# A second layer that takes unscaled rows, with the first modulation's gate steps moved to the first hybrid layer

## The chip, the core and the metric

The kernel runs on one core of one Trainium2 chip. The metric is the device time of one execution in microseconds (us), the median over runs. Everything is computed in float32; each large product is made of three fast ones, since both factors are split into a high half (rounded to fp32r) and a low half.

## The reference

256 rows of width 1024 go through four layers, each x + f(norm(x)) @ w_out, and a last norm. Layer 0 holds stick-breaking attention and an S5 mixer, layer 1 gated linear attention (GLA), layers 2 and 3 (the two hybrids) dilated attention and retention. What the change touches:

```python
def rms_norm(x, g):
    y = xf * lax.rsqrt(jnp.mean(xf * xf, axis=-1, keepdims=True) + EPS)
    return (y * g).astype(x.dtype)
# layer 1
h = rms_norm(x, odd_norm_g[i]);  proj = h @ odd_w_in[i]
q, k, v, z, r = jnp.split(proj, ...)
log_a = jax.nn.log_sigmoid(r @ gla_w_gate[i] + gla_b_gate[i]) / GLA_TAU
o = rms_norm(gla_chunked(q, k, v, log_a), gla_o_norm_g[i])
x = x + (o * jax.nn.silu(z)) @ odd_w_out[i]
# hybrids l = 0, 1
shift, scale, gate = jnp.split(c_act @ w_ada[l] + b_ada[l], 3)
h = rmsnorm(x, norm_w[l]) * (1 + scale) + shift
...
return x + gate * (merged @ w_out[l])
```

The factor of rms_norm is one number per row (token), so rows that aren't multiplied by it give products that can be multiplied by it afterwards.

## The kernel before

**Tiles and stream.** The 256 rows are two tiles (ti 0, 1) of 128 partitions. All weights come as one stream of 306 pieces, each two k-chunks of 128 rows by up to 512 columns (512 KB). SyncE loads piece n into RAW (five buffers) once the low half of piece n-5 is made; ScalarE (ACT) makes the high half WH (`hi(n)`, three buffers, after piece n-3 is read by TensorE), VectorE (DVE) the low half WL = RAW - WH (`lo(n)`, L1514); TensorE (PE) multiplies: for each chunk and row tile three matmuls of 512 columns (L598 to L600; L607 to L610 where the result is wanted turned). `half(time)` is one chunk of a piece, and time = 2n and 2n+1 are the steps by which everything else is placed: each engine's program is written out by hand as a loop over time, and the AT_ tables say at which step a side operation stands in it. hi and lo run two pieces ahead (AHEAD). Pieces 0 to 53 are layer 0, 54 to 89 layer 1, 90 to 197 and 198 to 305 the hybrids; the first pieces of layer 1 are `zr` (54 to 57, 336 columns), then gv0, gv1, gk, gq, z0, z1.

**From layer to layer.** The last three pieces of a layer (`closing`) run row tile by row tile (`split_half`, L636 to L638), so tile 0 is complete three halves ahead of tile 1; the first three pieces of the next (`opening`) do the same. In between, for each tile, DVE adds the product to X (`residual`, L2088), ACT squares X with a sum (`square`, L1091, which writes its squares to TK), DVE computes the factor NR by an inverse square root of 9 or 10 small dependent instructions (`rstd`, L1558 to L1574), DVE and GpSimd (POOL) multiply X by it into HN, which is TK (`scaled`, L1579, L2344), PE transposes HN (`norm_turn`, L699, four blocks to a bank), ACT takes the high halves HTh out of PSUM with the norm's weight as scale (`turned`, L1040) and DVE the low ones HTl (`turned`, L1590). The order on ACT and DVE is that of their `next_layer`, on PE that of `open_layer`.

**Modulations.** The hybrids' scale and shift columns are 16 dot products on DVE for each (`dot`, L1904, over w_ada_t, loaded by SyncE into two buffers): for the first hybrid at the steps AT_ADA0 in layers 0 and 1, for the second at AT_DOT1 in the first hybrid. The gate row is made of 16 gate steps on POOL (`ada`: load 256 KB, L2352, multiply, L2364 or L2366, add, L2368), at AT_ADA0 too for the first, at AT_ADA1 in the second hybrid for the second. After 8 steps each, PE sums over partitions with a matmul by ones (`ada_sum`, L812) and DVE adds the bias (`ada_out`, L1914).

**Layer 1's results.** ACT takes r (16 columns) and tanh(z/2) out of the zr banks, v out of gv0 and gv1, tanh(z/2) out of z0 and z1; DVE takes k and q with the decays; `gla_values` on ACT takes squares and copies of o (L1288), and DVE makes the norm of o (gr) and multiplies (`gla_gate`, L1979). In the hybrids DVE's `att_scores` (L2030 to L2037), ACT's `att_exp` and PE's `att_turn` (L900) follow one another for each of four heads, at steps 73 to 95.

## Time and profile before

| | |
|---|---|
| median of 3 runs | 1065.96 us (1065.74 to 1066.08) |
| the profiled execution | 1067.14 us |
| its span, first to last instruction | 1065.3 us |
| mean granted TensorE clock | 0.988 |
| busy: PE | 1017.6 us (96%) |
| busy: DVE, ACT, POOL | 708.7, 557.8, 205.2 us |
| DMA moved | 192.15 MB, mean 180 GB/s |

A busy PE isn't a PE at its peak, since matmuls overlap; but an idle PE is time lost wherever the chain that ended last runs through it. So the profile is read for the places where PE waits, and for what each of those waits hangs on.

### The profile page before, as it was taken

How to read it: one execution, taken by the hardware profiler on the slowest of the kernel's cores; microseconds unless marked ns; L12 is line 12 of the kernel's file. 1: busy time of each engine (PE TensorE's matmuls, PEld its weight loads, DVE VectorE, ACT ScalarE, POOL GpSimd, SP SyncE). 2: the span in 40 equal slices, each digit the busy share in tenths (PEclk: the TensorE clock that was granted, in tenths of full speed). 3: DMA queues.
4: the chain of work that ended last, by engine and by line, in shares of the span. 5: the costliest groups of instructions: out<-in, count | busy, mean ns of one | idle time of the engine just before them, and what ended most of it. 6: DMA issues, size and time to landing. Idle time of an engine off the chain costs nothing.

```text
span 1065.3 us, 15218 instructions
## 1 busy us (share of the span) xinstructions
PE 1017.6 (96%) x6020; PEld 891.8 (84%) x6020; DVE 708.7 (67%) x1113; ACT 557.8 (52%) x859; POOL 205.2 (19%) x212
## 2 busy tenths in 40 slices
PE   6999999989999899999999999989999999999996
PEld 5778889767977679998899888867999888998884
DVE  7984847978859656775566586664444565667666
ACT  6668577447435555445553345455444555334543
POOL 5800160423431100000004100020466000320000
PEclk9999999999999899999999999999999999999998
DMA  7543435758854568974466545545777446654651
GB/s 260 180 127 109 139 100 163 277 175 268 253 174 159 189 178 290 306 253 119 138 180 177 158 142 184 188 137 167 234 236 240 123 119 178 183 153 141 195 179 39
DMA packets 95350, 192.15 MB, mean 180 GB/s; under 512 B 8576, under 2 KB 11904, under 8 KB 95280
## 3 DMA queue, kind: packets, MB, share of 16 engines
q1 hardware_dynamic: 91008, 178.08, 54.2%
q0 software_dynamic: 3408, 11.18, 3.1%
q10 hardware_dynamic: 864, 1.93, 0.5%
q8 instruction: 47, 0.77, 0.3%
q14 instruction: 23, 0.19, 0.1%
HBM read 189.59 MB, written 1.05 MB: 179 GB/s over the span
## 4 chain that ended last, share of the span: by engine, by line
PE 83%; DVE 11%; ACT 3%; issue 2%; DMA 0%; DVEq 0%; ACTq 0%
PE G L598 14%; PE G L600 14%; PE G L599 14%; PE G L607 8%; PE G L610 8%; PE G L609 8%; DVE WL L1514 3%; PE B L561 2%; DVE AR L1904 1%; PE G L636 1%; PE G L638 1%; PE G L637 1%; ACT WH L1040 1%; PE B L900 1%; DVE SM L1572 1%
## 5 line engine op out<-in xcount | busy, mean ns | idle before, releaser
L1514 DVE TENSOR_TENSOR WL<-RAW,WH 128x1024 fp32r<-128x1024 f32 (+2 forms) x306 | 383.6, 1256 | 249.7 <-ACT WH L1040 248.7
L1040 ACT ACTIVATE WH<-RAW 128x1024 fp32r<-128x1024 f32 (+2 forms) x306 | 320.2, 1050 | 288.0 <-PE G L600 150.6
L598 PE MATMUL G<-WH,HTh 128*128 128x512 f32 (+1 forms) x564 | 228.3, 405 | 9.8 <-DVE WL L1514 9.5
L607 PE MATMUL G<-HTh,WH 128*128 128x256 f32 x768 | 219.5, 286 | 0.3 <-DVE HTl L1590 0.3
L600 PE MATMUL G<-WL,HTh 128*128 128x512 f32 (+1 forms) x564 | 218.4, 387 | 0.0
L609 PE MATMUL G<-HTl,WH 128*128 128x256 f32 x768 | 218.0, 284 | 0.0
L610 PE MATMUL G<-HTh,WL 128*128 128x256 f32 x768 | 217.9, 284 | 0.0
L599 PE MATMUL G<-WH,HTl 128*128 128x512 f32 (+1 forms) x564 | 217.5, 386 | 0.0
L607 PEld LDWEIGHTS G<-HTh,WH 128*128 128x128 f32 x768 | 147.7, 192 | 1.7 <-issue 1.5
L609 PEld LDWEIGHTS G<-HTl,WH 128*128 128x128 f32 x768 | 147.7, 192 | 0.4 <-issue 0.2
L610 PEld LDWEIGHTS G<-HTh,WL 128*128 128x128 f32 x768 | 147.6, 192 | 0.0
L598 PEld LDWEIGHTS G<-WH,HTh 128*128 128x128 f32 x564 | 106.2, 188 | 34.2 <-DVE WL L1514 11.6
L600 PEld LDWEIGHTS G<-WL,HTh 128*128 128x128 f32 x564 | 105.9, 188 | 21.8
L599 PEld LDWEIGHTS G<-WH,HTl 128*128 128x128 f32 x564 | 106.4, 189 | 18.4 <-issue 0.5
L2386 POOL TENSOR_TENSOR AR<-AR 128x256 f32<-128x256 f32 x16 | 18.2, 1139 | 318.4 <-DVE AR L2000 317.2
L598 PE MATMUL G<-WH,YTh 128*128 128x512 f32 x184 | 74.2, 404 | 2.5 <-DVE WL L1514 2.5
L600 PE MATMUL G<-WL,YTh 128*128 128x512 f32 x184 | 72.5, 394 | 0.0
L599 PE MATMUL G<-WH,YTl 128*128 128x512 f32 x184 | 72.3, 393 | 0.0
L1040 ACT ACTIVATE AR<-B 128x512 f32<-128x512 f32 (+5 forms) x83 | 43.0, 546 | 46.3 <-PE B L945 22.4
L2352 POOL DMA_DIRECT2D AR<-in_w_ada_g x32 | 18.7, 584 | 170.4 <-PE G L610 61.9
L1904 DVE CUSTOM_DVE_ANT_0 AR<-AR,CB,SM 128x1024 f32<-128x1024 f32 x32 | 48.9, 1528 | 2.8 <-DMA AR<-in_w_ada_t 2.8
L2368 POOL TENSOR_TENSOR AR<-AR 128x512 f32<-128x512 f32 x28 | 49.9, 1781 | 2.3
(344 smaller groups left out, 1320.5 us busy)
## 6 DMA issues: line engine op xcount, KB each, us to landing
RAW<-in_w_in SPq DMA_DIRECT2D x176, 512.0 KB, 3.8
RAW<-in_even_w_in SPq DMA_DIRECT2D x40, 512.0 KB, 3.7
AR<-in_w_ada_t SPq DMA_DIRECT2D x32, 512.0 KB, 4.8
AR<-in_w_ada_g POOLq DMA_DIRECT2D x32, 256.0 KB, 4.0
RAW<-in_odd_w_in SPq DMA_DIRECT2D x16, 512.0 KB, 4.2
RAW<-in_w_proj_ret SPq DMA_DIRECT2D x16, 512.0 KB, 3.5
RAW<-in_w_out SPq DMA_DIRECT2D x16, 512.0 KB, 3.6
RAW<-in_even_w_out SPq DMA_DIRECT2D x12, 512.0 KB, 4.3
```

Of the source, the lines that this page charges most:

```text
L561: ins = nc.tensor.transpose(ps[:, 128 * k:128 * k + 128], src(ti, j), IDENT)
L598: nc.tensor.matmul(o, xh, wh, start=begins, stop=False)
L599: nc.tensor.matmul(o, xl, wh, start=False, stop=False)
L600: ins = nc.tensor.matmul(o, xh, wl, start=False, stop=ends)
L607: nc.tensor.matmul(o, fh, h_[:, kx, :], start=begins and f % 2 == 0, stop=False, skip_group_check=True)
L609: nc.tensor.matmul(o, fh, l_[:, kx, :], start=False, stop=False, skip_group_check=True)
L610: ins = nc.tensor.matmul(o, fl, h_[:, kx, :], start=False, stop=ends and f % 2 == 1, skip_group_check=True)
L1040: return nc.scalar.activation(out_, ps, ACT.Copy, **kw)
L1514: vt(wl, raw, wh.bitcast(F32), ALU.subtract).then_inc(*dve.mark(LO, n))
L1904: nc.vector.tensor_tensor_reduce(w, w, CB[:, :], 0.5, co[f"b_ada{l}"][:, i:i + 1], ALU.mult, ALU.add, dst).then_inc(*dve.mark(DOT, l, i))
L2352: nc.gpsimd.dma_start((ADA2 if l else ADA)[:, i % 2, :], wv[:, i % 8, 512 * (i // 8):512 * (i // 8) + 512]).then_inc(s_ada[i % 2], 16)
L2368: gtt(acc, acc, w, ALU.add).then_inc(*pool.mark(ADA_P, l, i))
```

## The change

Layer 1 takes X as it is. `norm_turn(1, ...)` transposes X, right behind the residual sums; three of its four groups move into layer 0's last steps (AT_TURN1: after the halves 105, 106 and 107), the fourth behind the first half of layer 1. The squares, both `rstd` and a new `rows` (which makes NR squared, R2, and half of NR, HR) come at the end of `next_layer(1)` on ACT and DVE, ahead of lo(57) on DVE. The factor comes in where results leave PSUM: as scale of the copies of r, of tanh(z/2) and of v (there squared, for v and for k), of the squares and copies of o (for q), and once more in gr (for z). `scaled(1)` is gone on DVE and POOL, and with it TK as a stage.

The 16 gate steps of the first modulation and their two `ada_sum` go from layers 0 and 1 to the first hybrid, every fifth step from 25, sums at 63 and 104; the second modulation's dots there go from every third step to every fifth. The first modulation's dots stay (AT_DOT0 is the old AT_ADA0). The loads of ATM, DEC and GATE1, which ACT issued at the end of layer 1, and that of GATE0, which SyncE issued in layer 0, are issued by SyncE at step 12 of the first hybrid. POOL's three loads GM, RES and WGT, which followed `scaled(1)`, now wait until piece 55 is read. The gate steps' buffers are the second modulation's for both.

```diff
 AT_GLU_OUT = (89, 90)
-AT_ADA0 = (82, 86, 90, 94, 98, 112, 116, 120) + tuple(130 + 4 * i for i in range(8))
-AT_ADA0_SUM = {126: 4, 164: 5}
+AT_DOT0 = (82, 86, 90, 94, 98, 112, 116, 120) + tuple(130 + 4 * i for i in range(8))
 
...
+AT_DOT1 = tuple(27 + 5 * i for i in range(16))
+AT_ADA = [tuple(25 + 5 * i for i in range(16)), tuple(26 + 3 * i for i in range(16))]
+AT_ADA_SUM = [{63: 4, 104: 5}, {50: 4, 74: 5}]
+AT_LATE = 12
 AT_CB = 78
+AT_TURN1 = {105: (0, 0), 106: (0, 1), 107: (1, 0)}
+UNSCALED = (1,)
 
 
 
...
 
 
-        AH = Arena(2048)
-        DOT0 = AH.take(2, 1024)
-        ADA = AH.take(2, 512)
-        ADACC = AH.take(512)
...
                 pe.wait_ge(l_ci, 16)
-                pe.wait_ge(*(HN_P if q else HN_V).of(l, ti))
+                if l in UNSCALED:
+                    pe.wait_ge(*(RES_V.of(l - 1, ti, q) if l else (l_x[ti], 16)))
+                else:
+                    pe.wait_ge(*(HN_P if q else HN_V).of(l, ti))
                 for j in range(4):
                     c = 512 * q + 128 * j
-                    ins = nc.tensor.transpose(ps[:, 128 * j:128 * j + 128], HN[:, ti, c:c + 128], IDENT)
+                    ins = nc.tensor.transpose(ps[:, 128 * j:128 * j + 128], (X if l in UNSCALED else HN)[:, ti, c:c + 128],
+                                              IDENT)
                 ins.then_inc(*told("nt", l, ti, q))
 
             def open_layer(l, first):
 
-                for q in range(2):
-                    norm_turn(l, 0, q)
+                if l not in UNSCALED:
+                    for q in range(2):
+                        norm_turn(l, 0, q)
                 for i in range(6):
                     half(first + i)
-                    if i in (1, 2):
+                    if l in UNSCALED and i == 0:
+                        norm_turn(l, 1, 1)
+                    if l not in UNSCALED and i in (1, 2):
                         norm_turn(l, 1, i - 1)
 
...
                 half(time)
+                if time in AT_TURN1:
+                    norm_turn(1, *AT_TURN1[time])
                 if time in AT_S5["near"]:
                     s5_near(AT_S5["near"].index(time))
...
-                        ada_sum(1, AT_ADA1_SUM[216 * l + time])
+                    if time in AT_ADA_SUM[l]:
+                        ada_sum(l, AT_ADA_SUM[l][time])
                     if time in AT_ATT["scores"]:
                         att_scores(l, AT_ATT["scores"].index(time))
...
+                if l in UNSCALED:
+                    turned(l, 0, 0)
+                    turned(l, 0, 1)
+                    hi(n0)
+                    turned(l, 0, 2)
+                    turned(l, 0, 3)
+                    hi(n0 + 1)
+                    turned(l, 1, 0)
+                    turned(l, 1, 1)
+                    hi(n0 + 2)
+                    turned(l, 1, 2)
+                    turned(l, 1, 3)
+                    for ti in range(2):
+                        for n in range(2):
+                            square(l - 1, ti, n)
+                    return
                 square(l - 1, 0, 0)
...
                         act.wait_ge(*act.prev)
-                    nc.scalar.activation(LA[:, 0, :], ps[:, 256 * j:256 * j + 256], ACT.Square,
+                    nc.scalar.activation(LA[:, 0, :], ps[:, 256 * j:256 * j + 256], ACT.Square, scale=NR[1][:, ti:ti + 1],
                                          accum_out=gsq[:, i:i + 1]).then_inc(*act.tick())
                 junk = act.prev
-                copy(O1[:, ti, 512 * h2:512 * h2 + 512], ps[:, :]).then_inc(*act.mark(GLA_O, ti, h2))
+                copy(O1[:, ti, 512 * h2:512 * h2 + 512], ps[:, :], scale=NR[1][:, ti:ti + 1]).then_inc(*act.mark(GLA_O, ti, h2))
                 act.prev = junk
 
...
                         act.wait_ge(*tile(name, ti))
-                        copy(R16[:, ti, :], ps[:, 320:336]).then_inc(*act.mark(GLA_R, ti))
-                        silu_half(name, SZ[:, ti, 704:1024], ps[:, 0:320], ti)
+                        act.wait_ge(*ROWS.of(1))
+                        copy(R16[:, ti, :], ps[:, 320:336], scale=NR[1][:, ti:ti + 1]).then_inc(*act.mark(GLA_R, ti))
+                        silu_half(name, SZ[:, ti, 704:1024], ps[:, 0:320], ti, HR[1][:, ti:ti + 1])
                     elif name in ("gv0", "gv1"):
                         b = int(name[2])
-                        bank_out(V1[:, ti, 512 * b:512 * b + 512], ps[:, :], name, ti)
+                        bank_out(V1[:, ti, 512 * b:512 * b + 512], ps[:, :], name, ti, scale=R2[:, ti:ti + 1])
                     elif name in ("z0", "z1"):
                         b = int(name[1])
-                        silu_half(name, SZ[:, ti, 352 * b:352 * b + 352], ps[:, 0:352], ti)
+                        silu_half(name, SZ[:, ti, 352 * b:352 * b + 352], ps[:, 0:352], ti, HR[1][:, ti:ti + 1])
 
             def evac2(name):
...
             act.wait_ge(*side("yt", "gla", 2))
-            nc.scalar.dma_start(ATM, const("attmask").rearrange("p (a b) -> p a b", a=2)).then_inc(l_atm, 16)
-            nc.scalar.dma_start(DEC, const("decay").rearrange("p (a b) -> p a b", a=4)).then_inc(l_dec, 16)
-            nc.scalar.dma_start(GATE1, t["b_ada_2"][1, 2048:3072].rearrange("(a n) -> a n", a=1).partition_broadcast(
-                P)).then_inc(l_g1, 16)
...
 
+            def rows(l):
+
+                dve.wait_ge(*RSTD.of(l, 1))
+                if l == 1:
+                    vt(R2, NR[1], NR[1], ALU.mult)
+                ts(HR[l], NR[l], 0.5, None, ALU.mult).then_inc(*dve.mark(ROWS, l))
+
...
                 n0 = (0, 54, H0[0], H0[1])[l]
+                if l in UNSCALED:
+                    residual(l - 1, 0, 0)
+                    residual(l - 1, 0, 1)
+                    turned(l, 0, 0)
+                    turned(l, 0, 1)
+                    residual(l - 1, 1, 0)
+                    lo(n0)
+                    turned(l, 0, 2)
+                    turned(l, 0, 3)
+                    residual(l - 1, 1, 1)
+                    lo(n0 + 1)
+                    turned(l, 1, 0)
+                    turned(l, 1, 1)
+                    lo(n0 + 2)
+                    turned(l, 1, 2)
+                    turned(l, 1, 3)
+                    rstd(l, 0)
+                    rstd(l, 1)
+                    rows(l)
+                    return
                 residual(l - 1, 0, 0)
                 residual(l - 1, 0, 1)
...
-                if time in AT_ADA0_SUM:
-                    ada_out(0, AT_ADA0_SUM[time])
                 if time == AT_GLA["scan"]:
                     gla_scan()
-                if time in AT_ADA0:
-                    dot(0, AT_ADA0.index(time))
+                if time in AT_DOT0:
+                    dot(0, AT_DOT0.index(time))
                 if time in AT_GLA["scores"]:
                     gla_scores(AT_GLA["scores"].index(time))
...
                     rstd8(gr, gsq, 1.0 / 256)
+                    dve.wait_ge(*dve.prev)
+                    vt(gr.rearrange("p (t h) -> p t h", t=2), gr.rearrange("p (t h) -> p t h", t=2),
+                       NR[1].unsqueeze(2).to_broadcast([P, 2, 4]), ALU.mult).then_inc(*dve.tick())
                     GLA_R_DONE[0] = dve.prev
                 for h in AT_GLA["gated"].get(time, ()):
                     gla_gate(h)
...
                     nc.gpsimd.dma_start(CB[:, :], t["c_2"].partition_broadcast(P)).then_inc(l_cb, 16)
-                if time == AT_ADA0[0] - 5:
-                    pool.wait_ge(*side("sbo", 1, 1))
-                    ada_load(0, 0)
-                if time in AT_ADA0:
-                    ada_step(time)
-            for ti in range(2):
-                scaled(1, ti)
+            pool.wait_ge(*read(groups["zr"]["at"] + 1))
             nc.gpsimd.dma_start(GM, const("glamask")).then_inc(l_gm, 16)
             nc.gpsimd.dma_start(RES, const("reset")).then_inc(l_res, 16)
...
-                    ada_step(time)
                 if time == AT_GLA["scores"][0]:
                     own()
                     nc.gpsimd.memset(ST[:, :, :].rearrange("p a b -> p (a b)"), 0.0).then_inc(*pool.mark(GLA_S0, "st"))
 
             pool.wait_ge(*side("yt", "gla", 2))
-            ada_load(1, 0)
+            ada_load(0, 0)
             for l in range(2):
                 for ti in range(2):
...
                             P)).then_inc(l_fw, 16)
-                    if 216 * l + step in AT_ADA1:
-                        i = AT_ADA1.index(216 * l + step)
+                    if step in AT_ADA[l]:
+                        i = AT_ADA[l].index(step)
                         pool.wait_ge(*read(time // 2 - 1))
                         if i < 15:
-                            ada_load(1, i + 1)
-                        ada(1, i)
+                            ada_load(l, i + 1)
+                        ada(l, i)
+                    if l == 0 and step == AT_ADA[0][15] + 4:
+                        pool.wait_ge(*ADA_P.of(0, 15))
+                        ada_load(1, 0)
             for ti in range(2):
                 x = X[:, ti, 0:512]
...
                         u_spread()
-                    if at_ == AT_ADA0[0] - 5:
+                    if at_ == AT_DOT0[0] - 5:
                         sp.wait_ge(*side("sbo", 1, 1))
-                        nc.sync.dma_start(GATE0, t["b_ada_2"][0, 2048:3072].rearrange(
-                            "(a n) -> a n", a=1).partition_broadcast(P)).then_inc(l_g0, 16)
                         dot_load(0, 0)
-                    if at_ == AT_ADA0[0] - 1:
+                    if at_ == AT_DOT0[0] - 1:
                         dot_load(0, 1)
-                    if at_ in AT_ADA0 and AT_ADA0.index(at_) < 14:
-                        dot_load(0, AT_ADA0.index(at_) + 2)
+                    if at_ in AT_DOT0 and AT_DOT0.index(at_) < 14:
+                        dot_load(0, AT_DOT0.index(at_) + 2)
                     step = at_ - 2 * H0[0]
+                    if step == AT_LATE:
+                        sp.wait_ge(*side("yt", "gla", 2))
+                        nc.sync.dma_start(ATM, const("attmask").rearrange("p (a b) -> p a b", a=2)).then_inc(l_atm, 16)
+                        nc.sync.dma_start(DEC, const("decay").rearrange("p (a b) -> p a b", a=4)).then_inc(l_dec, 16)
+                        for gate, l_g, l in ((GATE0, l_g0, 0), (GATE1, l_g1, 1)):
+                            nc.sync.dma_start(gate, t["b_ada_2"][l, 2048:3072].rearrange(
+                                "(a n) -> a n", a=1).partition_broadcast(P)).then_inc(l_g, 16)
                     if step == AT_DOT1[0] - 3:
                         dot_load(1, 0)
                         dot_load(1, 1)
```

## Rows read from the trace of the kernel before

**Rows 1.** The page, chain that ended last, share of the span by engine.
```profile
PE 83%; DVE 11%; ACT 3%; issue 2%; DMA 0%; DVEq 0%; ACTq 0%
```

**Rows 2.** PE's waits, whole span: waiter <- releaser: us in total, times, longest us.
```profile
PE B L699 <- DVE TK L1579: 15.0, 8, 8.6
PE G L598 <- DVE WL L1514: 12.0, 10, 2.6
```

**Rows 3.** PE's waits from 180 to 222 us, end of layer 0.
```profile
PE G L598 <- DVE WL L1514: 2.5, 3, 1.8
```

**Rows 4.** Instructions of lines L1514 and L1904: count, ns min/median/max, first and last start.
```profile
L1514 DVE TENSOR_TENSOR WL<-RAW,WH x306: 846/1225/2309, 10.8 to 1048.2; 128x1024 fp32r<-128x1024 f32 x147, 128x704 fp32r<-128x704 f32 x4, 128x672 fp32r<-128x672 f32 x2
...
L1904 DVE CUSTOM_DVE_ANT_0 AR<-AR,CB,SM x32: 1270/1279/2322, 191.7 to 473.7; 128x1024 f32<-128x1024 f32 x32
```

**Rows 5.** Windows of 2 us: PE, PEld, DVE, ACT, POOL busy; PEclk, DMA share, GB/s.
```profile
210.00:212.00 2.00, 1.46 (x4) 1.16 (x5) 2.00 (x3) 0.00 (x0) 0.00 (x0) 0.75 0.59 231
212.00:214.00 2.00, 2.00 (x6) 1.56 (x5) 1.97 (x3) 0.00 (x0) 0.00 (x0) 0.50 0.91 312
...
240.00:242.00 2.00, 2.00 (x10) 2.00 (x9) 0.30 (x2) 1.14 (x4) 0.00 (x0) 0.57 1.03 387
...
328.00:330.00 2.00, 1.54 (x11) 1.52 (x12) 2.00 (x5) 0.00 (x0) 0.00 (x0) 1.00 0.19 33
```

**Rows 6.** Timeline of layer 1's opening: start us, duration us, engine, line, operation.
```profile
226.74 0.14 DVE L1558 TENSOR_SCALAR SM<-SM 128x1 f32<-128x1 f32 x1
226.87 0.63 ACT L1091 ACTIVATE TK<-X 128x512 f32<-128x512 f32 x1
...
228.43 0.39 PE L638 MATMUL G<-WL,YTh 128*128 128x512 f32 x1
...
228.78 0.16 DVE L1574 SCALAR_TENSOR_TENSOR SM<-SM 128x1 f32<-128x1 f32 x1
...
229.38 0.68 DVE L2088 TENSOR_TENSOR X<-G,X 128x512 f32<-128x512 f32 x1
...
229.52 1.21 PE L699 MATMUL B<-CI,TK 128*128 128x128 f32 x8 [0.70 <-DVE TK L1579]
...
231.99 1.13 DVE L1590 SCALAR_TENSOR_TENSOR HTl<-B,SM,HTh 128x128 fp32r<-128x128 f32 x4 [1.17 <-ACT HTh L1040]
232.49 1.15 ACT L1040 ACTIVATE HTh<-B,SM 128x128 fp32r<-128x128 f32 x4
...
232.75 0.39 PE L636 MATMUL G<-WH,HTh 128*128 128x336 f32 x1 [2.02 <-DVE HTl L1590]
...
243.85 0.42 PE L598 MATMUL G<-WH,HTh 128*128 128x336 f32 x1
```

**Rows 7.** PE's waits from 260 to 350 us, layer 1's body.
```profile
PE G L598 <- DVE WL L1514: 3.1, 2, 2.6
```

**Rows 8.** Timeline of layer 1's body: before its longest wait, and around the second ada_sum.
```profile
319.93 2.31 DVE L1904 CUSTOM_DVE_ANT_0 AR<-AR,CB,SM 128x1024 f32<-128x1024 f32 x1
...
320.79 0.59 ACT L1040 ACTIVATE AR<-B 128x512 f32<-128x512 f32 x1
...
324.94 1.80 DVE L1979 SCALAR_TENSOR_TENSOR AR<-AR,SM 128x256 f32<-128x256 f32 x2
...
334.94 1.02 PE L812 MATMUL B<-AR,CI 128*128 128x512 f32 x2
...
336.03 0.40 PE L599 MATMUL G<-WH,YTl 128*128 128x512 f32 x1
```

**Rows 9.** Window from 380 to 440 us, first hybrid, columns as in rows 5.
```profile
380.00:440.00 60.00, 60.00 (x417) 56.27 (x416) 37.81 (x46) 30.74 (x37) 0.00 (x0) 1.00 0.83 272
```

**Rows 10.** Timeline: first head of the first hybrid, and L1514 beside a gate step in the second.
```profile
478.60 0.17 DVE L2037 TENSOR_SCALAR SM<-SM 128x2 f32<-128x2 f32 x1
...
481.06 1.14 PE L900 MATMUL B<-CI,AR 128*128 128x128 f32 x9
...
776.33 1.79 DVE L1514 TENSOR_TENSOR WL<-RAW,WH 128x1024 fp32r<-128x1024 f32 x1 [1.23 <-ACT WH L1040]
```

52 lines of the change are left out of this document (21 added, 31 removed).

## The prediction

> **What bounds the kernel now.** I read the page's chain first: 83% of the path is TensorE (PE) and 11% VectorE (DVE) [rows 1]. PE is busy nearly everywhere, so what counts is where it waits. The waits view puts 12.0 us on WL, DVE's low half of a weight piece, and 15.0 us on TK, the scaled rows [rows 2]; 8.6 us of that is the start of the program, which is untouched. Asked by stretch, PE's waits lie at the end of layer 0, in the opening of layer 1, at two places in layer 1's body, and in the openings of the two hybrids; from 380 to 700 us and from 740 to 1030 us there is none. The timeline then says what DVE did before each wait. The change touches three causes: GpSimd (POOL) slowing DVE, the norm's chain ahead of the transposes, and work that merely moves.
>
> **Part 1, the 16 gate steps leave layers 0 and 1.** The low-half subtraction L1514 has median 1225 ns and maximum 2309, the dot L1904 1279 and 2322 [rows 4]: about 1.05 us more for one that lies beside a POOL step. At the end of layer 0 this pushes DVE behind, and PE waits three times for WL between 202 and 211 us, 2.5 us in all, 1.8 the longest [rows 3]. One stretched dot lies ahead of the first wait, two dots and two subtractions ahead of the last: more than 4 us against the 2.5 that are needed, and the high halves that DVE reads are there by then. I take all 2.5 us. Behind the longest wait the granted clock is 0.75 and 0.50 in two rows of 2 us [rows 5]: PE at 1.2 instead of 2.4 GHz under dense matmuls; 0.25 x 2 + 0.50 x 2 = 1.5 us lost in these rows, and a tenth beyond them. Without the wait I expect no fall: 1.6 us. Layer 0 gives **4.1 us** (bounds: 2.0, should half the waits stay and the clock still fall once, and 4.3).
> In layer 1's body PE waits twice for WL, 3.1 us, the longer one 2.6 [rows 7]. Before that one DVE runs a dot from 319.93 for 2.31 us, though ACT's last copy of the GLA output (320.79 + 0.59) is done at 321.4; then the norm's chain, and two gate multiplications in 1.80 us [rows 8], where 128x512 in one takes 0.68 [rows 6], so about 0.9 for the two. Without POOL the dot is done at 321.2 and the chain starts 0.75 us earlier, the multiplications save 0.9, little is saved in the chain, and the new multiply of gr by NR adds 0.2 with its wait. The wait shrinks from 2.6 to about 1.0: **1.7 us** gained with 0.2 of the chain (0.7 to 2.6).
>
> **Part 2, the two sums ada_sum move.** Each delays the stream: L812 begins at 334.94 and the second weight matmul behind it at 336.03 [rows 8], 1.09 us where 0.23 is the pace: 0.86 us each. Hybrid 1 has no idle PE, so both are paid in full there: 1.7 us. The second one's place in layer 1 is dense, so 0.86 comes back. The first one's lies right ahead of the shorter WL wait (3.1 - 2.6 = 0.5 us), which hangs on DVE's scan; no POOL step touches that, and the wait grows by as much: nothing comes back. Net **0.9 us lost** (0 to 1.7).
>
> **Part 3, the opening of layer 1.** The closing's last matmul starts at 228.43 and is done by 228.8. Then rstd (L1558 at 226.74 to the end of L1574 at 228.94: 2.2 us), scaling, eight transposes (1.21 us), ACT's and DVE's halves; the first matmul of zr starts at 232.75, and that of piece 57, from where PE is dense, at 243.85 [rows 6]. In between lie a second norm chain, two more groups of transposes and lo(57). I lay out the new order with the durations of the same rows: residual 0.68, four copies 1.15 (ACT), four low halves 1.13 (DVE), four transposes 0.6, and 0.85 for lo, the minimum in [rows 4].
> - PE: two groups of transposes lie inside the closing and a third behind it, so the closing ends at 229.9 and the third group at 230.5.
> - ACT turns tile 0 from 226.7, so chunks 0 to 3 are there at 227.9; DVE's low halves end at 229.1, residual(1,0) at 229.8, lo(54) at 230.6. PE starts zr at 230.6 instead of 232.75.
> - DVE goes on: four low halves and residual(1,1) to 232.3 (the fourth group waits 0.9 us for it), lo(55) 233.1, four low halves, lo(56) 235.1, four low halves 236.2. PE has worked off pieces 54 to 56 by 238.8.
> - Only now the norm: ACT's four squares (0.63 and the read of the sum, 0.8 each) end at 237.4, DVE does both chains at 2.2 us and rows(): 241.0. Behind them in DVE's queue stands lo(57), done at 241.9, and PE behind that: a wait of **3.1 us** in place of those removed.
>
> Dense work starts at 241.9 instead of 243.85: 1.95 us earlier. The scalings that go (DVE's were in the chain counted above, POOL's lay beside them) cost nothing more, and the pointer scales of the evacuations are hidden: ACT takes zr out of PSUM at 244 or later, when ROWS (241.0) is long there; without that cover ACT's queue, and the high halves behind it, would wait for DVE. POOL's new wait for piece 55 holds only its three loads, which land by 243 and are first used behind piece 58: free. But before, the clock was down in the middle of the opening (0.57 in 240 to 242 [rows 5]), where PE partly waited anyway. Behind one 3.1 us wait I expect the fall in dense work, at the 1.5 us of part 1. Net **0.45 us** gained (1.95 without the fall; below nothing, -1, should the dense work meet more than one).
> The Trainium skill speaks against this part: "TensorE: Matmul & The Clock Gate", Part 1, says that the array's default is 1.2 GHz and that only activity releases it. By that rule the one long wait gives the 1.95 us back nearly whole. The rows behind the 1.8 us wait agree with it; behind the 2.6 us wait of layer 1 the clock is 1.00 [rows 5], which doesn't.
>
> **Part 4, hybrid 1 gets the gate steps, wider dots, and four loads on SP.** DVE is busy 37.81 of 60 us from 380 to 440 with PE at 60.00 [rows 9]. Dots (1.28 us) go from every third to every fifth step, gate steps add at most 1.1 us to an instruction per five steps: DVE's load stays about the same, and I cost it at nothing (0 to 2). What hides it is DVE's lead of two pieces; with that gone each stretched instruction would be paid by PE. In hybrid 2, where gate steps run beside the same pieces, L1514 takes at worst 1.79 us [rows 10] and PE waits for nothing. In the attention the chain is tighter: DVE's negated maxima at 478.60, then ACT's exponentials, then PE's transposes at 481.06 [rows 10], of which ACT leaves about 0.6 us of margin, four times. Gate steps and dots now fall into it; their bound is the rival below.
> The Trainium skill ("SBUF — State Buffer", Who interferes with whom) says that DVE contends with GpSimd where two of its inputs come from SBUF, and not with one. By that the score steps, which read PSUM, and the reductions keep their length and only a subtraction or a dot ahead of them stretches. No row here shows a gate step beside them.
> ATM, DEC and both gates (384 + 3 x 512 KB, 1.9 MB) now stand ahead of piece 14 in SP's queue. At the 387 GB/s of [rows 5] they are 5 us. Five buffers at 2.75 us a piece, less the two halves, leave some 11 us from issue to use, and a piece lands in 4: hidden, with 2 us to spare. Where they stood before, ACT had nothing to do but wait for the closing: nothing gained.
>
> **Sum.** 4.1 + 1.7 + 0.45 - 0.9 = 5.35 us. The profiled execution took 1067.14 us with a span of 1065.3; the median of the runs is 1065.96. The sum is made on the profiled one and taken off the median: 1065.96 - 5.35 = **1060.6 us**.
>
> **Rivals.**
> - *The clock doesn't fall in dense work.* For it: none behind the 2.6 us wait. Against: the 1.8 us one. 1060.6 - 1.5 = 1059.1.
> - *The attention chain loses its margin.* A subtraction or dot stretched by 1.1 us, less 0.6 of margin, at most four times: 1062.6. For it: steps 75, 80, 85 and 90 lie in the heads. Against: DVE idles between heads.
> - *The opening gives nothing and SP's burst delays piece 14.* lo(57) 2 us later than laid out and 1 us of load unhidden: 1063.6. For it: everything in the opening hangs on one queue, DVE's. Against: each duration has its row.
> - *Slower: POOL beside the dots costs hybrid 1 what it cost layer 0.* Three gate steps cost 4.1 us there, 1.4 each; 16 cost 22: 1060.6 + 22 = 1082, and a quarter of that is no change (1066). It decides from the point where DVE falls more than its two pieces behind. Against it: DVE at 63% there, and at 2.00 of 2 us in the row at 210 [rows 5].
>
> **How the numbers follow.** Forecast 0.50; no fall 0.20; attention 0.14; opening 0.10; slower hybrid 0.06. The range 1057.5 to 1063.5 takes in the first three with their bounds, and leaves out the outer ends. A measurement of this kernel tells about 0.2% (2.1 us) from no change, so faster means below 1063.8: the first three cases and half of the fourth, 0.88; the rest of it and a mild form of the last are no change, 0.08; slower 0.04.
>
> **What would show it.** Right: no PE wait on WL and the clock at 1.00 from 195 to 215; the waits on TK in layer 1 gone, and a WL wait of some 3 us ahead of piece 57, behind two norm chains; one near 1.3 us at the scan and one near 1.0 before z1; hybrid 1 longer by 1.7 us. Wrong: PE waits in hybrid 1, a layer 0 that keeps its waits though POOL is gone, or an opening as long as before.

## The result and the profile of the changed kernel

The changed kernel takes 1058.68 us (median; 1057.71 to 1060.37) where the kernel before takes 1065.74 (1063.55 to 1066.08): a ratio of 0.9937, with a 95% interval from 0.9923 to 0.9951. Run again later it stood at 1059.74 against 1065.89, ratio 0.9934 [0.9910, 0.9957]. The forecast was 1060.6 in a range of 1057.5 to 1063.5; the sign and the range hold, and the gain is 7.1 us instead of 5.35. The execution whose trace is read below took 1058.27 us with a span of 1056.4 (before: 1067.14 and 1065.3), so the two traces differ by 8.9 us, 1.8 more than the medians. Where that comes from is a finding of its own.

The page's chain by engine, and TensorE's (PE's) waits over the whole span (waiter, what it waited for: us in total, times, longest us), changed kernel; they answer to [rows 1, 2]. L599, L608 and L637 are the stream's matmuls here, L1535 is the low half, L703 a transpose.

```profile
PE 85%; DVE 9%; ACT 3%; issue 1%; DMA 1%; SPq 0%; DVEq 0%; ACTq 0%
```

```profile
PE B L703 <- DVE TK L1607: 13.5, 6, 8.6
PE G L599 <- DVE WL L1535: 10.8, 9, 2.4
...
PE G L608 <- DVE WL L1535: 1.1, 1, 1.1
...
PE B L703 <- DVE X L2136: 0.5, 1, 0.5
```

The totals hide what moved. At the end of layer 0 (180 to 226 us) the view is empty: [rows 3]'s 2.5 us are gone. One wait of 2.4 us on WL is new, in the opening of layer 1, and so is one of 1.1 us for L608, in the first hybrid.

Windows of 2 us of the changed kernel (busy PE, PEld, DVE, ACT, POOL; PEclk, DMA share, GB/s), to be held against [rows 5]:

```profile
208.00:210.00 2.00, 2.00 (x10) 1.68 (x9) 1.61 (x3) 0.64 (x1) 0.00 (x0) 1.00 0.86 304
210.00:212.00 2.00, 2.00 (x10) 1.65 (x10) 0.61 (x1) 1.06 (x1) 0.00 (x0) 1.00 1.05 390
...
240.00:242.00 2.00, 2.00 (x12) 1.52 (x10) 2.00 (x3) 0.99 (x2) 0.00 (x0) 1.00 0.95 376
...
358.00:360.00 2.00, 2.00 (x8) 1.60 (x8) 0.27 (x1) 0.26 (x1) 0.00 (x0) 0.50 0.43 168
```

At 210 DVE was busy all 2.00 us in the kernel before and is now busy 0.61, with PE at 2.00 and the clock at 1.00. The clock is also 1.00 at 240, behind the new wait. Apart from the last piece of the span, only the stretch from 356 to 362 records a fall.

The opening of layer 1 in the changed kernel, timeline (start us, us, engine, line, operation), with DVE's rows and then PE's:

```profile
226.23 0.68 DVE L2136 TENSOR_TENSOR X<-G,X 128x512 f32<-128x512 f32 x1
...
230.44 0.14 DVE L1579 TENSOR_SCALAR SM<-SM 128x1 f32<-128x1 f32 x1
...
234.91 0.60 DVE L2226 TENSOR_SCALAR SM<-SM 128x2 f32<-128x2 f32 x1
234.98 0.85 DVE L1535 TENSOR_TENSOR WL<-RAW,WH 128x672 fp32r<-128x672 f32 x1
```

```profile
227.06 0.63 PE L703 MATMUL B<-CI,X 128*128 128x128 f32 x4 [0.53 <-DVE X L2136]
235.89 0.42 PE L599 MATMUL G<-WH,HTh 128*128 128x336 f32 x1 [2.40 <-DVE WL L1535]
```

The two chains of the norm and the small row work run from 230.44 with PE's pieces 54 to 56 beside them; the fourth low half starts at 234.98 behind them, and PE is dense from 235.89. That is the layout of the prediction's part 3, one row after the other.

**The stages of every trace.** To see where time goes I took the start of the same six matmuls of the stream in each trace: one near the end of layer 0 (214.19 us in the kernel before), one well inside layer 1 (260.88), one in its closing (355.89), one behind the opening of hybrid 1 (377.88), one at the end of hybrid 1 (696.25), and the last one with WH in the stream (1054.34). Each column is the time from one of them to the next; "layer 0" is the time from the start of the span to the first. A "fall" is a run of windows with the recorded clock below 1; adding (1 - clock) x 2 us over its rows gives 1.7 us each time, for all of them. A run of twice that length counts as two. The last column says where those ahead of the last 20 us lie. The kernels in the lower rows are those of the experiments.

| kernel | layer 0 | opening | body of layer 1 | opening of hybrid 1 | hybrid 1 | rest | falls, at us |
|---|---|---|---|---|---|---|---|
| before | 214.2 | 46.7 | 95.0 | 22.0 | 318.4 | 358.1 | 210, 238, 360, 368, 708 |
| changed | 209.4 | 43.1 | 92.0 | 21.3 | 321.4 | 358.1 | 356 |
| changed again (e9) | 210.9 | 44.6 | 92.1 | 21.8 | 320.2 | 358.1 | 52, 62, 236, 360 |
| gates only (e1) | 209.4 | 45.0 | 91.6 | 20.4 | 324.3 | 358.0 | 228, 350, 404 |
| gates late (e10) | 210.9 | 46.1 | 91.6 | 20.4 | 320.2 | 358.1 | 62, two from 228 |
| norm only (e2) | 211.7 | 46.6 | 96.6 | 21.4 | 318.4 | 359.4 | two from 238, 326, 366, 714 |
| before, light (e3) | 211.0 | 46.1 | 92.5 | 20.4 | 318.5 | 358.1 | 62, two from 230, two from 700 |
| norm, light (e12) | 209.4 | 43.1 | 93.0 | 21.8 | 318.4 | 358.1 | 356, 698 |
| changed, light (e4) | 209.4 | 44.6 | 92.1 | 21.8 | 320.1 | 358.1 | 234, 358 |
| long wait (e5) | 211.0 | 47.3 | 92.1 | 21.8 | 320.1 | 358.1 | 62, 240, 362 |
| late dots (e6) | 209.4 | 43.1 | 92.1 | 21.3 | 320.2 | 358.1 | 356, two from 698 |
| late dots (e11) | 209.3 | 44.6 | 92.1 | 21.8 | 320.2 | 358.1 | 234, 358 |
| low half first (e7) | 210.9 | 44.4 | 92.0 | 22.0 | 320.2 | 359.0 | 62, 240, 358, 710 |
| both (e8) | 209.4 | 44.4 | 92.1 | 20.4 | 320.2 | 358.1 | 236, 350 |

Between kernels that are alike in a stage it repeats to 0.1 us but for falls and one wait in hybrid 1, so a stage of one trace can be read against that of another, while whole times can't.

### The profile page after: what moved, and what is told of

Same layout as the page of the kernel before. It is cut to its first block, busy times and chain, and to the rows that moved or that the text cites. A ratio compares the mean times of both kernels' runs of the same rounds, so it can differ in the third digit from the quotient of the medians.

```text
span 1056.4 us, 15216 instructions
## 1 busy us (share of the span) xinstructions
PE 1010.3 (96%) x6020; PEld 887.2 (84%) x6020; DVE 699.5 (66%) x1114; ACT 559.8 (53%) x859; POOL 204.8 (19%) x210
## 4 chain that ended last, share of the span: by engine, by line
PE 85%; DVE 9%; ACT 3%; issue 1%; DMA 1%; SPq 0%; DVEq 0%; ACTq 0%
PE G L599 15%; PE G L601 15%; PE G L600 15%; PE G L608 8%; PE G L611 8%; PE G L610 8%; DVE WL L1535 3%; PE B L562 2%; PE G L637 1%; PE B L908 1%; PE G L639 1%; DVE SM L1593 1%; PE G L638 1%; DVE HTl L1618 1%; PE B L730 1%
## 5 line engine op out<-in xcount | busy, mean ns | idle before, releaser
L1535 DVE TENSOR_TENSOR WL<-RAW,WH 128x1024 fp32r<-128x1024 f32 (+2 forms) x306 | 384.1, 1258 | 253.3 <-ACT WH L1048 252.4
L599 PE MATMUL G<-WH,HTh 128*128 128x512 f32 (+1 forms) x564 | 228.1, 404 | 11.0 <-DVE WL L1535 10.8
L608 PE MATMUL G<-HTh,WH 128*128 128x256 f32 x768 | 219.7, 286 | 1.3 <-DVE WL L1535 1.1
L608 PEld LDWEIGHTS G<-HTh,WH 128*128 128x128 f32 x768 | 147.5, 192 | 3.2 <-issue 1.8
L599 PEld LDWEIGHTS G<-WH,HTh 128*128 128x128 f32 x564 | 106.1, 188 | 35.1 <-DVE WL L1535 12.1
L601 PEld LDWEIGHTS G<-WL,HTh 128*128 128x128 f32 x564 | 105.8, 188 | 21.8
L599 PE MATMUL G<-WH,YTh 128*128 128x512 f32 x184 | 72.9, 396 | 0.0
L1048 ACT ACTIVATE AR<-B 128x512 f32<-128x512 f32 (+5 forms) x79 | 40.7, 544 | 45.5 <-PE B L953 22.4
L1952 DVE CUSTOM_DVE_ANT_0 AR<-AR,CB,SM 128x1024 f32<-128x1024 f32 x32 | 42.1, 1317 | 3.9 <-DMA AR<-in_w_ada_t 3.9
```

Source lines behind the costliest of these rows:

```text
L599: nc.tensor.matmul(o, xh, wh, start=begins, stop=False)
L601: ins = nc.tensor.matmul(o, xh, wl, start=False, stop=ends)
L608: nc.tensor.matmul(o, fh, h_[:, kx, :], start=begins and f % 2 == 0, stop=False, skip_group_check=True)
L1048: return nc.scalar.activation(out_, ps, ACT.Copy, **kw)
L1535: vt(wl, raw, wh.bitcast(F32), ALU.subtract).then_inc(*dve.mark(LO, n))
L1952: nc.vector.tensor_tensor_reduce(w, w, CB[:, :], 0.5, co[f"b_ada{l}"][:, i:i + 1], ALU.mult, ALU.add, dst).then_inc(*dve.mark(DOT, l, i))
```

## The experiments

### Which half carries the gain (e1, e2)

e1 keeps the gate half and puts layer 1's norm back:

```diff
-AT_TURN1 = {105: (0, 0), 106: (0, 1), 107: (1, 0)}
-UNSCALED = (1,)
+AT_TURN1 = {}
+UNSCALED = ()
...
-            pool.wait_ge(*read(groups["zr"]["at"] + 1))
+            for ti in range(2):
+                scaled(1, ti)
```

(with every scale by NR, HR and R2, and the multiply of gr, taken out). e2 does the reverse:

```diff
-AT_DOT1 = tuple(27 + 5 * i for i in range(16))
+AT_DOT1 = tuple(27 + 3 * i for i in range(16))
...
+            for time in range(2 * groups["zr"]["at"], 2 * H0[0] - 6):
+                if time in AT_ADA0:
+                    ada_step(time)
```

(gate steps, sums and the four loads in their old places).

> The gate half of the change alone: the first modulation's gate steps in the first hybrid, its dots, sums and loads where the changed kernel has them, but layer 1's norm as before (scaled rows, 16 transposes of HN, two halves of scaling each on VectorE and GpSimd). Theory of the prediction (GpSimd's gate steps stretch the dots and low halves beside them): layer 0 gains what the changed kernel gained there, 4.8 us by its end (the waits of 2.5 us and the clock fall gone), the body of layer 1 about 2 more with the sum that moved away, and hybrid 1 gives 1.2 + 0.9 + 0.9 back: 4.8 + 2.9 - 3.0, some 4.5 us below the kernel before, near 1061.2 us (1060.2 to 1062.3). Rival (the gains of layer 0 come from the shorter sequence of the norm, not from the gate steps): layer 0 as before, and the kernel is 1 us slower than before, 1066.7 us.

> The norm half of the change alone: layer 1 takes unscaled rows and the factor comes in where results leave PSUM, the gate steps, dots, sums and loads of the first modulation stay where they were. The opening of layer 1 gains 3.1 us as in the changed kernel, if the two halves are independent, and the layer-0 waits and the low clock of their windows stay: 1062.6 us (1061.6 to 1063.6). If the two halves only work together (the gate steps that still run in the opening hold up its 128x128 low halves and rows), it gains under 1 us: 1065 us. The recorded clock between 210 and 212 us should stay below 1 as in the kernel before.

Measured: the gate half alone 1057.91 us (1057.27 to 1061.61), ratio 0.993 [0.9911, 0.9948], which is the whole gain of the changed kernel, and 3.3 us below the expected 1061.2. Its layer 0 ends at 209.4 as in the changed kernel, so the rival is out; what the expectation lacked are the opening (46.7 to 45.0), the opening of hybrid 1 (22.0 to 20.4) and 1.4 us more in the body (95.0 to 91.6, where 2 were expected). Its trace is the slowest of its six runs (1061.61 us): hybrid 1 has a wait of 2.4 us and a fall there, of which more below. The norm half alone takes 1068.41 us (1065.42 to 1069.69), ratio 1.0017 [1.0004, 1.0029]: no gain, rather a loss, where 3 us were expected. Its trace has a longer wait ahead of the first dense piece, and two falls right behind it. The expected low clock between 210 and 212 us is missing, though the gate steps are still there: at the end of layer 0 PE waits once, for 2.0 us, and every window from there to 238 us stands at 1.00, so layer 0 takes 211.7 us and not 214.2. PE's waits of the norm half alone from 226 to 262 us, and windows:

```profile
PE G L602 <- DVE WL L1544: 3.2, 1, 3.2
```

```profile
200.00:204.00 4.00, 2.04 (x10) 1.35 (x8) 3.96 (x4) 3.16 (x4) 2.70 (x3) 1.00 0.56 200
...
208.00:212.00 4.00, 4.00 (x19) 3.31 (x18) 4.00 (x5) 1.28 (x2) 3.92 (x2) 1.00 0.88 267
...
238.00:240.00 2.00, 1.10 (x4) 1.10 (x5) 2.00 (x3) 0.00 (x0) 1.90 (x2) 0.52 0.99 356
240.00:242.00 2.00, 2.00 (x9) 2.00 (x8) 2.00 (x2) 0.17 (x1) 0.00 (x0) 0.50 0.68 215
242.00:244.00 2.00, 2.00 (x7) 1.71 (x6) 2.00 (x5) 1.85 (x5) 1.02 (x2) 0.50 0.86 216
244.00:246.00 2.00, 2.00 (x8) 1.56 (x8) 1.86 (x3) 0.31 (x1) 1.92 (x2) 0.77 0.97 347
```

What follows: the two halves don't add up. The gate half makes the norm half harmless, and the norm half adds nothing that the medians show.

### Is it GpSimd's arithmetic? (e3, e4, e12)

The same edit in three kernels: each gate step of the first modulation keeps its load, its waits and its place, but multiplies and adds 1 column of 512; the other 511 columns of the first hybrid's gate are left out. e3 makes it in the kernel before, e12 in the norm half alone, e4 in the changed kernel.

```diff
             def ada(l, i):
...
+                if l == 0:
+                    w, acc = w[:, 0:1], acc[:, 0:1]
```

> The kernel before with its loads, waits and order unchanged, but GpSimd's multiply and add of each gate step of the first modulation work on 1 column of 512; the other 511 columns of that layer's gate are left out of the computation. If it is the time that GpSimd's elementwise work overlaps VectorE's which stretches dots and low halves (the prediction's reason for +4.1 in layer 0), the waits of TensorE ahead of low halves in layer 0 go, and with them the clock fall: -4.8 us there and -1.5 to -2 in layer 1's body, 1059.4 us (1058.5 to 1060.5). Rival (the gate's loads, or the order of the queues, cause the waits): no change, 1065.7 us.

Measured: 1057.32 us (1056.54 to 1059.37), ratio 0.9920 [0.9904, 0.9937], 2.1 us better than expected. Instructions of lines L1514 and L1904 in this kernel (count, ns min/median/max), against [rows 4]:

```profile
L1514 DVE TENSOR_TENSOR WL<-RAW,WH x306: 845/1225/2052, 10.8 to 1040.4; 128x1024 fp32r<-128x1024 f32 x147, 128x704 fp32r<-128x704 f32 x4, 128x672 fp32r<-128x672 f32 x2
...
L1904 DVE CUSTOM_DVE_ANT_0 AR<-AR,CB,SM x32: 1271/1278/1285, 192.8 to 465.9; 128x1024 f32<-128x1024 f32 x32
```

and its window at 210 us:

```profile
210.00:212.00 2.00, 2.00 (x11) 1.65 (x10) 1.23 (x2) 0.34 (x2) 0.00 (x0) 1.00 0.82 301
```

The slowest dot went from 2322 to 1285 ns although every load still runs, and the waits and the fall at the end of layer 0 are gone: the stage ends at 211.0, or 209.4 without the fall at 62 us that this execution happened to have (1.6 us). Of the low halves, the four that took about 2.3 us in the kernel before (203.37, 208.21, 249.74 and 289.25 us) are gone; the 2052 ns that is left starts at 49.48 us, ahead of all gate steps, and the kernel before has it too. Loads and queues are acquitted; GpSimd's elementwise work beside DVE's is the cause.

> The changed kernel with the same cut: GpSimd's multiply and add for the first modulation work on 1 column of 512 (511 columns of that gate left out), in the first hybrid now. It prices what the gate steps cost in their new place. In the changed kernel TensorE waits 1.1 us for one low half near 402 us, where a dot had waited 3.85 us for its load and three low halves took 5.04 us beside a GpSimd step. If the step's stretch is needed for that wait, it goes and the kernel gains 1.2 us: 1057.5 us. If the late load alone makes it, 1058.5 us. Everything else there is hidden under both, so no gain over 1.5 us; more would mean that the gate steps cost something in hybrid 1 which no wait showed.

Measured: 1058.82 us (1057.15 to 1060.41), ratio 0.993 [0.9911, 0.9949]: nothing gained over the changed kernel. The wait near 402 us is absent, and hybrid 1 takes 320.1 us. But the changed kernel's second trace (e9), with full gate steps, shows 320.2 and no such wait either. So 16 full gate steps cost hybrid 1 under 0.1 us where this wait doesn't come, and the wait doesn't belong to every execution. Whether the gate steps take part in it e4 can't tell, since its first dot stood idle for its load for 2.75 us only, where the trace with the wait has 3.85.

> The norm half alone, with GpSimd's gate steps of the first modulation on 1 column (511 of 512 columns of that gate left out), in their old place. The norm half alone stood 2.5 us above the kernel before in the medians (1068.4 against 1065.9), and it isn't known why. Its traces' falls of the clock suggest chance and a longer wait ahead of the first dense piece (3.2 us); the other candidate is that GpSimd's full gate steps, which now run on while DVE does the row work, stretch it. Without them: if the norm half is worth nothing of its own, this equals the kernel before with the same cut, 1057.3 us; if it gives the 1.4 us of the opening, 1055.9 us; if what slows the norm half alone has nothing to do with GpSimd's arithmetic, 1059.8 us, 2.5 above.

Measured: 1057.50 us (1056.67 to 1059.65), ratio 0.9923 [0.9906, 0.9940]. That is the first answer: with GpSimd's arithmetic out of the way the norm half is worth nothing (1057.50 against 1057.32). The norm half alone lost because of the arithmetic: taking it out gives 10.9 us there (1068.41 to 1057.50) and 8.6 in the kernel before (1065.88 to 1057.32). In the stages the wait ahead of the first dense piece is 2.4 us again instead of 3.2.

### What does the wait in the opening cost? (e5, e7)

e5 lengthens the two chains of the factor, in `rstd`:

```diff
-                for step in range(3):
+                last = 5 if l == 1 else 2
+                for step in range(last + 1):
```

> The changed kernel with three more Newton steps in each of the two chains for layer 1's row factor: 12 more tiny VectorE instructions of 219 and 160 ns with their gaps, about 2.6 us in all, so that TensorE's wait ahead of the first dense piece of layer 1 grows from 2.4 to about 5.0 us. The wait alone costs 2.6 us: 1061.3 us. The prediction reckoned that the clock falls in the dense work behind a wait of 3.1 us and took 1.5 us off for it; the changed kernel shows no fall behind 2.4 us. If a wait of this length does bring a fall in dense work, the windows behind it record a clock below 1 and the time is 1.5 us more again: 1062.8 us. If this place is proof against it, all windows stay at 1.00.

Measured: 1061.70 us (1061.62 to 1063.15), ratio 0.9959 [0.9946, 0.9971], 3.0 above the first median of the changed kernel and 2.0 above the second, and between the two expected times. PE's waits from 226 to 256 us, and windows, of this kernel:

```profile
PE G L599 <- DVE WL L1535: 5.1, 1, 5.1
```

```profile
236.00:238.00 2.00, 0.00 (x0) 0.00 (x0) 1.65 (x10) 0.29 (x1) 1.08 (x2) 1.00 0.88 281
238.00:240.00 2.00, 0.00 (x0) 0.00 (x0) 1.82 (x9) 0.00 (x0) 0.00 (x0) 1.00 0.27 107
240.00:242.00 2.00, 1.78 (x6) 1.78 (x7) 2.00 (x3) 0.00 (x0) 0.00 (x0) 0.51 0.37 48
242.00:244.00 2.00, 2.00 (x9) 1.96 (x9) 1.77 (x4) 0.86 (x4) 0.00 (x0) 0.64 0.96 343
```

The wait came out at 5.1 us, near the expected 5.0 (2.7 more), and one fall stands behind it. The opening is 47.3 us: 2.7 above the changed kernel's trace with one fall there (44.6). A wait of twice the length brings the same single fall as the short one does when it brings one.

e7 pulls the fourth low half ahead of the second chain, and the high half to match:

```diff
                     rstd(l, 0)
+                    lo(n0 + 3)
                     rstd(l, 1)
```

> The changed kernel with the fourth low half of layer 1's weights between VectorE's two chains of Newton steps, and its high half between ScalarE's squares. The prediction laid the opening out so that the two chains, 4.8 us, stand ahead of that low half and make the wait of TensorE (2.4 us in the changed kernel) ahead of the first dense piece. If so the wait shrinks to the time of one chain less, by up to 2.4 us, and the row factor is ready 1.2 us later, which the first results that leave PSUM may feel: 1056.7 us (1056.2 to 1057.8). If the wait is set by something else (the high half, the weights' load), the time stays at 1058.7 us.

Measured: 1058.14 us, but from 1055.84 to 1064.34, ratio 0.993 [0.9908, 0.9953]: no gain beyond the spread. The waits from 226 to 256 us in this kernel:

```profile
PE G L599 <- DVE WL L1537: 1.8, 1, 1.8
```

The wait wasn't taken away, it moved one piece on: the fifth low half now stands behind the second chain. The opening with one fall takes 44.4 us instead of 44.6. That points to DVE's total work as the limit of this stretch, and not to the order of one item; it isn't shown apart from that.

### Hybrid 1, and two versions that might beat both (e6, e8, e10, e11)

In the changed kernel's first trace PE waits 1.1 us near 402 us. DVE's and then POOL's rows there:

```profile
399.01 1.67 DVE L1952 CUSTOM_DVE_ANT_0 AR<-AR,CB,SM 128x1024 f32<-128x1024 f32 x1 [3.85 <-DMA AR<-in_w_ada_t]
...
400.61 5.04 DVE L1535 TENSOR_TENSOR WL<-RAW,WH 128x1024 fp32r<-128x1024 f32 x3
```

```profile
399.43 1.78 POOL L2415 TENSOR_SCALAR AR<-AR,SM 128x512 f32<-128x512 f32 x1
401.30 2.14 POOL L2417 TENSOR_TENSOR AR<-AR 128x512 f32<-128x512 f32 x1
```

The first dot of the second modulation waits 3.85 us for its load with two low halves ready behind it, and then dot and low halves run beside a gate step: 5.04 us for three, where three alone take 3.7. e6 moves the dots three half-pieces on and leaves the loads; e8 adds the edit of e7; e10 puts the later dots into the gate half alone; e11 is e6 once more.

```diff
-AT_DOT1 = tuple(27 + 5 * i for i in range(16))
+AT_DOT1 = tuple(30 + 5 * i for i in range(15)) + (103,)
...
-                    if step == AT_DOT1[0] - 3:
+                    if step == AT_DOT1[0] - 6:
```

> The changed kernel with the second modulation's dots three half-pieces later (the last one one half-piece earlier), its loads issued when they were. The first dot, which waited 3.85 us for its load at 399 us with the low halves queued behind it, finds the load landed, so VectorE doesn't fall behind there and TensorE's 1.1 us wait near 402 us goes: 1.1 us less, 1057.6 us. If that wait came from the stretch by GpSimd's gate steps and not from the load, it moves with the dot or stays: 1058.7 us.

> The two edits of the later dots and the earlier fourth low half together, as a version that may beat both kernels. The places are 160 us apart and share no queue in between, so the gains should add: 2.4 + 1.1 = 3.5 at the most, 2.5 likely: 1056.2 us (1055.0 to 1057.5).

Measured: 1057.72 us (1057.08 to 1059.56) and 1058.00 (1056.72 to 1058.99), ratios 0.9920 [0.9907, 0.9934] and 0.9918 [0.9904, 0.9933]. Neither stands apart from the changed kernel, and e8 misses its expected 1056.2. Both traces take 320.2 us in hybrid 1. That looks like the expected 1.1 us, until it is held against the unchanged kernel run once more:

> The changed kernel once more, word for word, beside the two below on the same chip. What is asked is which stretches record a clock below 1. The runs so far show falls of TensorE's clock that each take 1.7 us (3.4 us at half speed), at places that differ between executions of the same instructions: the changed kernel's first trace has none between 234 and 240 us, the one with one column of GpSimd work in hybrid 1 has one there, with the same wait of 2.4 us ahead. Theory (a fall behind these waits is a matter of chance): a time of 1057 to 1061 us, median near 1058.9, and falls at some other set of the same places (235 to 240, 356 to 362, 404 to 410, 700 to 710). Rival (the first trace is what the kernel does): the same single fall at 356 to 362 before the end, and 1058.3 us.

> The gate half alone (norm of layer 1 as before) with the second modulation's dots three half-pieces later. With the gate half alone the first dot's load came late too and TensorE waited 2.4 us near 404 us, with a fall behind it; that wait and the fall should go. If the norm half is worth nothing of its own, this equals the changed kernel with later dots, 1057.7 us or less; if the norm half is worth the 1.4 to 1.9 us that the opening of layer 1 shows in single traces, it stands 1.5 us above that, 1059.2 us.

> The changed kernel with the later dots once more, beside the unchanged one and the gate half on the same chip. The wait of 1.1 us near 402 us is absent from its trace and its gain of 1.1 to 1.3 us should stand in the medians: 1057.6 us against 1058.9 us. If chance of falls swamps it, the two medians lie within 0.5 us.

Measured side by side: changed kernel 1059.74 us (1057.23 to 1061.72), later dots 1059.00 (1057.46 to 1067.09), gate half with later dots 1058.26 (1057.44 to 1060.15). The gate half isn't 1.5 us above the later dots, as it would be if the norm half gave what the opening shows, but 0.7 below, and the later dots miss the expected gain of 1.3 us. The changed kernel word for word now has hybrid 1 at 320.2 us and no wait there. Its DVE rows at the same place:

```profile
401.67 1.28 DVE L1952 CUSTOM_DVE_ANT_0 AR<-AR,CB,SM 128x1024 f32<-128x1024 f32 x1 [3.03 <-DMA AR<-in_w_ada_t]
...
402.88 2.85 DVE L1535 TENSOR_TENSOR WL<-RAW,WH 128x1024 fp32r<-128x1024 f32 x2
```

DVE idles 0.8 us less for the load, the dot is as good as over when the gate step begins (402.91 us), and nobody waits. A stretched dot isn't needed for such a wait, though: in e1 the dot took 1.28 us behind 4.97 us of idling for its load, and PE waited 2.4 us. So the later dots can't be credited with a gain: of the traces with dots at their first place and full gate steps in hybrid 1 (changed, e1, e5, e7, e9) two have the wait, 1.1 and 2.4 us, and three don't. With later dots none of the four does (e6, e8, e10, e11), which is too few to call it cured, and the medians don't tell. Their dots now lie fully beside gate steps, and the first three of each trace take 2.31 to 2.33 us instead of 1.28; still PE waits for nothing there, which shows how much DVE's lead hides in this stage.

e9 has a fall at 236 us, behind the same 2.4 us wait that brought none in the first trace. Its windows:

```profile
236.00:238.00 2.00, 0.58 (x2) 0.58 (x3) 1.93 (x7) 0.21 (x1) 1.00 (x2) 0.81 0.90 303
238.00:240.00 2.00, 2.00 (x9) 2.00 (x8) 2.00 (x4) 0.00 (x0) 0.00 (x0) 0.50 0.92 266
```

A fall here comes or stays away between executions of the same instructions behind the same wait; what decides it no run shows, and it is treated as chance below. Nor does every fall cost time. e9 has one at 52 us that the first trace lacks, and from 57 us on its matmuls start as early: PE's next wait for a low half has shrunk by as much. The wait in the first trace, then in e9:

```profile
56.20 0.50 PE L599 MATMUL G<-WH,HTh 128*128 128x512 f32 x1 [1.59 <-DVE WL L1535]
```

```profile
56.13 0.58 PE L599 MATMUL G<-WH,HTh 128*128 128x512 f32 x1 [0.27 <-DVE WL L1535]
```

The 2.3 us between the spans of the two traces of the changed kernel (1056.4 and 1058.7) are falls and that one wait: layer 0 +1.5 (the fall at 62 us), opening +1.5, opening of hybrid 1 +0.5, hybrid 1 -1.2.

## Why the prediction was right, and where its terms were off

**Part 1, layer 0** (4.1 us predicted): 214.2 to 209.4, 4.8 us. The three waits went entirely and the fall with them, as said; the bound of 4.3 was too low, since the gain is 0.6 us more than the waits (2.5) and the recorded fall (1.7) together. The reason is that a wait in the view is less than the delay of the stream: the matmul at 202.58 us starts 0.95 us behind the one ahead of it, where 0.23 is the pace, so it is 0.72 us late for a wait of 0.56. Against the changed kernel the three waits put the stream 3.2 us back before the fall, and the fall 1.6 more up to the end of the stage (its last 0.15 us of cost lie behind it, in the next stage). Cause shown by e3: 4.8 us again with the loads left in, once its fall at 62 us is taken off. That a wait brings the fall is less sure than the prediction had it: of the two kernels with gate steps in layer 0, one has a fall behind its wait of 1.8 us, the other none behind 2.0 (e2); the twelve traces without their arithmetic there have neither wait nor fall.

**Part 1, body of layer 1** (1.7 us, and 0.86 from the second sum): 95.0 to 92.0, 3.0 us against 2.6. The named steps are there: the dot that took 2.31 us takes 1.28, two gate multiplications 0.87 us instead of 1.80, and the 2.6 us wait is 1.1. With the sum and the light gate steps (e3) the body takes 92.5; the norm half adds 0.5 to that (e12: 93.0) and takes the same off the changed kernel's gain (92.1 against 91.6 for the gate half alone). It lies in the wait ahead of z1, 1.1 us with the new norm and 0.6 without (e10). I had costed its multiply of gr at 0.2, and that is what it takes; the other 0.3 isn't explained.

**Part 2, the moved sums** (-0.9 us): hybrid 1 went from 318.4 to 320.2 us (e9; the first trace has 1.2 more, with its wait of 1.1), 1.8 against the 1.7 of two sums at 0.86. Kernels that leave the sums in layer 1 (e2, e3, e12) stay at 318.4 to 318.5. In layer 1 the first gave nothing back, since the wait for the scan grew from 0.5 to 1.3 us, and the second gave 0.88. This term was exact.

**Part 3, the opening** (0.45 us, or 1.95 without a fall): this was the step that failed in its size, by 1.6 us in either case. The stage went from 46.7 us to 43.1 without a fall and 44.6 with one, 3.6 or 2.1 us. The price of a fall in dense work, 1.5 us, is what the traces show (44.6 - 43.1). Mis-sized was the layout: counted from the end of layer 0, PE was dense 26.5 us in instead of the 27.7 of the layout (241.9 less 214.2), as against 29.7 before. DVE's chains started at 230.44, which is 21.1 us in where the layout has 22.0; the fourth group of transposes waited 0.5 us for its residual, not 0.9; and from the first chain to the first dense matmul 5.4 us passed, not 5.7. The wait was 2.4 us instead of 3.1. Behind the start of dense work the changed kernel gains another 0.4 us, between 243.85 and 249.08 us of the kernel before, in dense work; what held the kernel before there isn't resolved. The rival by which the opening gives nothing is out in every trace, since even the ones with a fall gain 2.1 us.
I had made the fall part of the forecast. Of the six traces with the 2.4 us wait, three have it (e4, e9, e11) and three don't (the first one, e6, e12); the waits of 1.8 (e7, e8) and 5.1 us (e5) have it too. So neither case was safe, and the trace that came first went by the rival "the clock doesn't fall in dense work". That this rival's 1059.1 us stands 0.4 from the median is luck: it had the opening 1.6 us too slow like the forecast. The Trainium skill ("TensorE: Matmul & The Clock Gate", Part 1) calls the number of slow matmuls at the start of a kernel variable from run to run. Of the start the traces here say nothing new; in the middle of the kernel they show the like, one and the same wait of 2.4 us, fall or no fall.

**But the norm half nets nothing.** The forecast gave the opening 0.45 us, and doubted it for the fall alone; what the norm half costs further on wasn't in it, but for the 0.2 of the multiply. By stages, falls included, the changed opening stands 1.9 us below the old one among kernels free of gate steps (old 45.0, 46.1, 46.1; new 43.1 or 44.6, three each, mean 43.9). It loses 0.5 in the body, and some 1.3 in the opening of hybrid 1, where its traces have 21.3 to 22.0 us with a fall at 356 to 362, and those of the old norm (e1, e3, e10) 20.4, with a fall at 350 or none; e8 is the exception on the new side, with 20.4 and its fall at 350. The sum is about zero, as the medians say. Why the falls of the new norm gather in that later stretch isn't settled.

**Part 4, hybrid 1** (0, bounds 0 to 2): right as a rule, since e4 with the arithmetic taken out is 0.05 us from e9 with it. The 1.1 us of the first trace lies within the bounds, but its mechanism, a dot that is late for its load, wasn't named, and the 2.4 us of e1, whose hybrid 1 is the same, lie outside them. The burst on SP's queue (up to 398 GB/s, from 384 to 388 us) delayed no weight piece so far that PE waited. Whether it makes the dot's load late isn't shown: without it DVE idles 2.5 to 2.9 us for that load (before, e2, e3, e12), with it 2.75 to 4.97 in six traces. The rival with the attention chain didn't come: no PE wait stands at steps 73 to 105. DVE's groups there, line, shapes and count, busy us and mean ns, in the changed kernel from 470 to 535 us:

```profile
L1535 DVE TENSOR_TENSOR WL<-RAW,WH 128x1024 fp32r<-128x1024 f32 x18 | 26.3, 1465 | 8.3 <-ACT WH L1048 8.3
...
L2078 DVE SCALAR_TENSOR_TENSOR AR<-B,AR 128x384 f32<-128x384 f32 x9 | 4.5, 551 | 6.1 <-PE B L899 6.1
```

and in the kernel before from 478 to 543 us:

```profile
L1514 DVE TENSOR_TENSOR WL<-RAW,WH 128x1024 fp32r<-128x1024 f32 x18 | 22.0, 1224 | 17.0 <-ACT WH L1040 17.0
L2030 DVE SCALAR_TENSOR_TENSOR AR<-B,AR 128x384 f32<-128x384 f32 x9 | 4.5, 550 | 8.7 <-PE B L891 8.7
```

The low halves are 240 ns longer in the mean beside gate steps and dots, the score steps, which read PSUM, are as long as before; one group of three at 465.92 us lies inside a gate step (464.80 to 467.10) and takes 1.49 us like its neighbours. That agrees with the rule of the Trainium skill ("SBUF — State Buffer", Who interferes with whom) for which the prediction had no row. DVE's idle time took the stretch up: 17.0 us ahead of these low halves before, 8.3 now.

**Slower rival** (1082 us): out. It would have needed DVE more than two pieces behind in hybrid 1; the 320.2 us of that stage hold the two sums and nothing else.

**The sum again.** From the stages, with one fall in the opening and one at the opening of hybrid 1: 4.8 + 2.1 + 3.0 + 0.2 - 1.8 = 8.3 us against the trace of before, which itself stood 1.2 us above its median with five falls. Taken off the median, as the prediction did with its sum, this gives about 1057.7, and off the time of that trace 1058.8, 0.2 from the measured one. So the terms together were 3 us too small (8.3 against 5.35), and the base, which took the sum off a median while the waits and the fall were read from a slower execution, hides 1.2 of it. The chances have a slip as well: by the prediction's own cases "faster" adds up to 0.89, not 0.88.
